# Seven norms of a two-block kernel: squares summed with a token per partition, the row spread by a matmul with the identity

## The reference, cut to what matters

```python
def rms_norm(x, g):
    xf = x.astype(jnp.float32)
    y = xf * lax.rsqrt(jnp.mean(xf * xf, axis=-1, keepdims=True) + EPS)
    return (y * g.astype(jnp.float32)).astype(x.dtype)
```

## Time and profile before

| | |
|---|---|
| median of three runs | 2040.0 us |
| the profiled execution | 2036.15 us |
| its span in the profile | 2034.4 us |
| PE busy, DVE, ACT, POOL | 1922.1, 991.6, 758.7, 111.9 us |
| mean granted clock of PE | 0.981 of full |
| read from HBM | 280.84 MB, 139 GB/s over the span |

### The profile page before, as it was taken

How to read it: one execution, slowest core, us unless ns; L and a number is a source line. 1 busy time by engine, 2 the same in 40 slices (tenths; PEclk the granted TensorE clock), 3 DMA queues, 4 the chain that set the end, 5 groups by cost and what they waited for, 6 DMA issues and landing times.

```text
span 2034.4 us, 28356 instructions
## 1 busy us (share of the span) xinstructions
PE 1922.1 (94%) x11844; PEld 1661.3 (82%) x11844; DVE 991.6 (49%) x1126; ACT 758.7 (37%) x918; POOL 111.9 (6%) x106
## 2 busy tenths in 40 slices
PE   7999998899997999888999999999989989989998
PEld 6989896798985768767887788887867767989997
DVE  5555465554556426664233522223245475554454
ACT  5334435433444424164222412213234435344343
POOL 3000201200022000000000100000001010000000
PEclk9999999999998999899999999999999999999999
DMA  9996387498433312001323232332324211556641
GB/s 255 323 309 233 116 310 254 141 335 259 176 124 125 116 59 85 19 1 62 104 83 103 62 103 83 103 103 83 103 78 153 73 62 49 180 145 180 183 176 61
DMA packets 288755, 283.47 MB, mean 139 GB/s; under 512 B 8760, under 2 KB 265669, under 8 KB 282515
## 3 DMA queue, kind: packets, MB, share of 16 engines
q1 hardware_dynamic: 287312, 279.56, 43.6%
q0 software_dynamic: 1120, 2.46, 0.4%
q10 hardware_dynamic: 227, 0.06, 0.0%
HBM read 280.84 MB, written 1.07 MB: 139 GB/s over the span
## 4 chain that ended last, share of the span: by engine, by line
PE 84%; DVE 8%; ACT 5%; POOL 1%; issue 1%; DMA 1%; ACTq 0%; SPq 0%; DVEq 0%
PE PS L1516 24%; PE PS L1518 23%; PE PS L1517 23%; PE PS L1612 2%; PE PS L1601 2%; PE PS L2007 1%; DVE WLO L951 1%; PE PS L1861 1%; PE PS L1995 1%; PE PS L1957 1%; PE PS L1970 1%; ACT WHI L591 1%; DVE RT L989 1%; POOL X L546 1%; ACT PB L860 1%
## 5 line engine op out<-in xcount | busy, mean ns | idle before, releaser
L1516 PE MATMUL PS<-AHI,WHI 128*128 128x256 f32 (+1 forms) x2480 | 801.1, 323 | 45.8 <-DVE ALO L1217 18.6
L1517 PE MATMUL PS<-ALO,WHI 128*128 128x256 f32 (+1 forms) x2480 | 787.8, 318 | 0.0
L1518 PE MATMUL PS<-AHI,WLO 128*128 128x256 f32 (+1 forms) x2480 | 787.3, 317 | 0.0
L951 DVE TENSOR_TENSOR WLO<-RAW,WHI 128x2048 fp32r<-128x2048 f32 x210 | 485.0, 2311 | 431.3 <-ACT WHI L591 431.3
L1516 PEld LDWEIGHTS PS<-AHI,WHI 128*128 128x128 f32 x2480 | 480.6, 194 | 114.5 <-issue 51.8
L591 ACT ACTIVATE WHI<-RAW 128x2048 fp32r<-128x2048 f32 x210 | 400.4, 1908 | 284.5 <-PE PS L1518 266.8
L1517 PEld LDWEIGHTS PS<-ALO,WHI 128*128 128x128 f32 x2480 | 481.2, 194 | 30.3 <-issue 1.7
L1518 PEld LDWEIGHTS PS<-AHI,WLO 128*128 128x128 f32 x2480 | 480.5, 194 | 29.0
L1516 PE MATMUL PS<-SHI,WHI 128*128 128x256 f32 (+1 forms) x704 | 221.3, 314 | 2.3 <-DVE HB L1493 2.3
L1518 PE MATMUL PS<-SHI,WLO 128*128 128x256 f32 (+1 forms) x704 | 218.0, 310 | 0.0
L1517 PE MATMUL PS<-SLO,WHI 128*128 128x256 f32 (+1 forms) x704 | 217.9, 310 | 0.0
(11 more groups left out here) (248 smaller groups left out, 1723.2 us busy)
## 6 DMA issues: line engine op xcount, KB each, us to landing
RAW<-in_w_in_dram SPq DMA_DIRECT2D x98, 512.0 KB, 4.5
MRAW<-in_w_mod_dram SPq DMA_DIRECT2D x48, 1024.0 KB, 7.2
RAW<-in_ffn_w_gu_dram SPq DMA_DIRECT2D x88, 512.0 KB, 7.6
RAW<-in_w_gate_up_dram SPq DMA_DIRECT2D x88, 512.0 KB, 5.0
RAW<-in_ffn_w_down_dram SPq DMA_DIRECT2D x44, 512.0 KB, 4.3
RAW<-in_w_down_dram SPq DMA_DIRECT2D x44, 512.0 KB, 4.0
RAW<-in_w_out_dram SPq DMA_DIRECT2D x24, 512.0 KB, 4.6
RAW<-in_w_o_attn_dram SPq DMA_DIRECT2D x16, 512.0 KB, 4.2
```

The lines of the kernel that those rows point to most:

```text
L951: dve.tensor_tensor(WLO[:, c % RING, :], RAW[:, c % RING, :], WHI[:, c % RING, :].bitcast(F32), ALU.subtract)\
L1516: pe.matmul(out, whi, xhi, start=first, stop=False, skip_group_check=shared)
L1517: pe.matmul(out, whi, xlo, start=False, stop=False, skip_group_check=shared)
L1518: return pe.matmul(out, wlo, xhi, start=False, stop=last, skip_group_check=shared)
```

## The change

For norms 3, 7, 8, 9, 10, 11 and 12 (`ROW_BANK`):
- `norm_sums` makes the squares the stationary operand and one column of ones the moving one, once per block of 128 tokens. The sums land in PSUM as 128x2 or 128x4 numbers, a token per partition. Per k that is two or four one-column matmuls instead of one of 256 or 512 columns.
- `norm_std` takes the root of these numbers into the new tile `RTOK`, `norm_row` their reciprocal.
- PE spreads the result (`norm_rows`): per block of tokens a matmul with `RTOK`'s column, repeated over 128 columns, as the stationary operand and the identity as the moving one. It waits for the reciprocal, and stands right behind the last sums in PE's order, in norm 3 ahead of the sixteen modulation matmuls.
- DVE waits for the spread and reads the row from PSUM (`rms_row`) in its products. In norms 8 to 10 ACT copies the context's row to `RT` for POOL; the second reciprocal after the seventh product is gone, and so are the two separate roots.

The other six norms stay as they were.

```diff
+ROW_BANK = {3: 0, 7: 3, 8: 6, 9: 6, 10: 6, 11: 6, 12: 6}
+CTX_BANK = {8: 5, 9: 7, 10: 7}
+ROWS_DONE = {n: i + 1 for i, n in enumerate(ROW_BANK)}
...
+        RTOK = sm("RTOK", [P, 4])
...
+        def rms_row(n_norm):
+
+            return PS[:, ROW_BANK[n_norm], 0:TX] if n_norm in ROW_BANK else RT[:, 0:TX]
...
             def norm_std(n_norm, t):
 
                 act.wait_ge(S("n_ss"), n_norm + 1)
-                act.activation(RT[:, 0:P * t], stat_row(n_norm, t), ACT.Sqrt, scale=1.0 / D, bias=EPSC[:, 0:1])\
-                   .then_inc(S("n_std"), 1)
+                if n_norm in ROW_BANK:
+                    act.activation(RTOK[:, 0:t], PS[:, STAT_BANK[n_norm], 0:t], ACT.Sqrt, scale=1.0 / D, bias=EPSC[:, 0:1])\
+                       .then_inc(S("n_std"), 1)
+                else:
+                    act.activation(RT[:, 0:P * t], stat_row(n_norm, t), ACT.Sqrt, scale=1.0 / D, bias=EPSC[:, 0:1])\
+                       .then_inc(S("n_std"), 1)
+                if n_norm in CTX_BANK:
+
+                    act.wait_ge(S("n_bc"), ROWS_DONE[n_norm])
+                    act.activation(RT[:, TX:TB], PS[:, CTX_BANK[n_norm], 0:TX], ACT.Copy).then_inc(S("n_rtc"), 1)
...
             def norm_row(n_norm, t):
 
                 dve.wait_ge(S("n_std"), n_norm + 1)
+                if n_norm in ROW_BANK:
+                    dve.reciprocal(RTOK[:, 0:t], RTOK[:, 0:t]).then_inc(S("n_rt"), 1)
+                    dve.wait_ge(S("n_bc"), ROWS_DONE[n_norm])
+                    return
...
             def modulated(n_norm, inst, a_inst, which, shift, t):
 
                 halves = t // 2
-                if halves == 1:
-                    norm_row(n_norm, t)
-                else:
-                    dve.wait_ge(S("n_stdx"), inst + 1)
-                    dve.reciprocal(RT[:, 0:TX], RT[:, 0:TX]).then_inc(S("n_rt"), 1)
-                    dve.wait_ge(S("n_rt"), n_norm + 1)
+                norm_row(n_norm, t)
...
-                                             in1=RT[:, 0:TX], op0=ALU.mult, op1=ALU.mult).then_inc(S("xm"), 1)
-                    if k == 6 and halves == 2:
-                        dve.wait_ge(S("n_std"), n_norm + 1)
-                        dve.reciprocal(RT[:, TX:TB], RT[:, TX:TB]).then_inc(S("n_rtc"), 1)
+                                             in1=rms_row(n_norm), op0=ALU.mult, op1=ALU.mult).then_inc(S("xm"), 1)
...
                 for k in ks:
                     pe.wait_ge(S("n_sq"), KT * n_norm + k + 1)
-                    last = pe.matmul(stat_row(n_norm, t), ONES[:, :], src[:, k, 0:P * t], start=k == 0, stop=k == KT - 1)
+                    if n_norm in ROW_BANK:
+                        for a in range(t):
+                            last = pe.matmul(PS[:, STAT_BANK[n_norm], a:a + 1], src[:, k, a * P:a * P + P], ONES[:, 0:1],
+                                             start=k + a == 0, stop=k == KT - 1, skip_group_check=True)
+                    else:
+                        last = pe.matmul(stat_row(n_norm, t), ONES[:, :], src[:, k, 0:P * t], start=k == 0, stop=k == KT - 1)
...
+            def norm_rows(n_norm):
+
+
+                t = n_stat(n_norm)
+                pe.wait_ge(S("n_rt"), n_norm + 1)
+                for a in range(t):
+                    bank = ROW_BANK[n_norm] if a < 2 else CTX_BANK[n_norm]
+                    last = pe.matmul(PS[:, bank, a % 2 * P:a % 2 * P + P], RTOK[:, a:a + 1].broadcast_to([P, P]), IDENT[:, :],
+                                     start=True, stop=True)
+                last.then_inc(S("n_bc"), 1)
...
                 norm_sums(3, 2, SQ1, range(4, KT))
+                norm_rows(3)
                 modulation(32, 33, 34, 35)
```

More of the change, by code:

```diff
@@ L750, in modulated @@
                 squares(lambda k: X[:, k, 0:n], lambda k: SQ2[:, k, 0:n], ready, range(squared, KT))
[L751 to L756, removed]
-                else:
-                    norm_std(n_norm, t)
+                norm_std(n_norm, t)
                 for k in range(KT):
@@ L997, in gained_lo, with branch @@
                        .then_inc(S("act_lo"), 1)
-            def branch(src, gain, inst=None, name=None):
+            def branch(src, gain, n_norm, inst=None, name=None):
                 for k in range(KT):
-                    dve.scalar_tensor_tensor(out=TU[:, k, :], in0=src(k), scalar=gain(k), in1=RT[:, 0:TX],
+                    dve.scalar_tensor_tensor(out=TU[:, k, :], in0=src(k), scalar=gain(k), in1=rms_row(n_norm),
                                              op0=ALU.mult, op1=ALU.mult).then_inc(S("xt"), 1)
@@ L1080, in _ @@
                 dve.wait_ge(S("hg"), 2)
-                branch(lambda k: acc(k, TX), lambda k: HG[:, inst, k:k + 1], *((1, "attn_pre_g"), (4, "ple_pre_g"))[inst])
+                branch(lambda k: acc(k, TX), lambda k: HG[:, inst, k:k + 1], post, *((1, "attn_pre_g"), (4, "ple_pre_g"))[inst])
                 if inst == 1:
@@ L1177, in _ @@
                 dve.wait_ge(S("f_ev"), 4)
-                branch(lambda k: FB[:, k, :], lambda k: par("attn_post_g", k), 3, "ffn2_pre_g")
+                branch(lambda k: FB[:, k, :], lambda k: par("attn_post_g", k), 3, 3, "ffn2_pre_g")
             split_w(None, FIRST["ple_proj"] + AHEAD)
@@ L1201, in _ @@
             dve.wait_ge(S("f_ev"), 8)
-            branch(lambda k: FB[:, k, :], lambda k: par("ple_post_g", k))
+            branch(lambda k: FB[:, k, :], lambda k: par("ple_post_g", k), 7)
             split_w(None, FIRST["ple_gate"] + 3 + AHEAD)
@@ L1503, in _ @@
             for k in range(KT):
-                dve.scalar_tensor_tensor(out=YF[:, k, :], in0=X[:, k, 0:TX], scalar=par("norm_final_2", k), in1=RT[:, 0:TX],
+                dve.scalar_tensor_tensor(out=YF[:, k, :], in0=X[:, k, 0:TX], scalar=par("norm_final_2", k), in1=rms_row(12),
                                          op0=ALU.mult, op1=ALU.mult).then_inc(S("yf"), 1)
@@ L1827, in _ @@
             norm_sums(7, 2, SQ1, range(2, KT))
+            norm_rows(7)
             for layer in range(2):
@@ L1865, in _ @@
                 norm_sums(8 + 2 * layer, 4, SQ2, range((0, 6)[layer], KT))
+                norm_rows(8 + 2 * layer)
                 beside = [lambda: network(0), lambda: network(1), lambda: network(2), lambda: taps(0), lambda: taps(1),
@@ L2071, in _ @@
                 norm_sums(9 + 2 * layer, nt // P, SQ2, range(4, KT))
+                norm_rows(9 + 2 * layer)
                 inst = 2 + layer
@@ L2088, in _ @@
             norm_sums(12, 2, SQ1, range(6, KT))
+            norm_rows(12)
             pe.wait_ge(S("xd"), 3 * KT)
```

## The result

The changed kernel takes 2047.64 us (median of 6 runs, 2046.37 to 2051.43) beside 2039.21 us for the kernel before, timed beside it: a ratio of 1.0047, with a 95% interval of 1.0037 to 1.0057. It is slower by 8.4 us. The forecast was 2045 us (2031 to 2053), 4.8 us more than before, with a half chance of slower.

A forecast was written before the change was run, and what follows sets the result against it. TensorE, busy 94% of the span, was taken as the bound. The norms' terms (-2.6+3.6+2.4+2.5-0.5-0.6) summed to +4.8 us: 2041.0 for the profiled execution, 2045 us against the median, range 2031 to 2053.

The forecast's parts named there:

- main mechanism: One-column sums hardly hold or lift TensorE's clock; norm 8's would run at half throughout, 13.1 us against 9.07.
- The chain: Root to first product in a norm: 1.34 us for two tiles (0.95 gained), 1.77 for four (0.5 gained).
- Sums equal at full clock: At full clock, one-column matmuls per k take the same time as the old wide one: nothing gained or lost.
- Norm 3: Shorter chain, and faster products and adds with the row in PSUM: -2.6 us; -0.9 if only the chain counts.
- Norms 7 and 8: Norm 7 -0.3; norm 8's sums at half clock +4.0, its spread +0.3, the rest -0.4: +3.6 us together.
- Norm 9: Low clock behind the first sum batch +2.5, slow spread +0.2, second reciprocal gone -0.3: +2.4 us.
- Norm 10: Low clock where sums alternate with down-projection +3.2, chain and second reciprocal -0.7: +2.5 us.
- rival (b): Clock fails only in norm 8; norm 9's first batch and norm 10's alternation hold it: -0.9 us, 2039; 22%.
- Rival (c): Norm 10's clock stays down until the stage ends, 13 us instead of one or two stretches: 2053; 8%.
- Norms 11 and 12: Norm 11: shorter chain less a longer low stretch, -0.5 us; norm 12: shorter chain without cover, -0.6 us.
- Rival (a): One-column work keeps the clock, so all seven norms gain: -10.5 us, 2029.5; 20%.
- Rival (d): The row in PSUM doesn't speed VectorE: norm 3 -0.9 instead of -2.6 us; no chance of its own given.

The follow-up runs named there:

- w128_all: The changed kernel with all seven norms' sums multiplied by 128 columns of ones instead of one; 2030.4 us, 7.8 us faster than the kernel before.
- narrow_8: w128_all with norm 8's sums alone back to one column; that stage cost 5.2 us more than in w128_all.
- narrow_7: w128_all with norm 7's sums alone back to one column; 2.3 us more than w128_all over the stage of norms 7 and 8.
- w128_8: The changed kernel with 128 columns of ones in norm 8's sums alone; gained 5.8 us by the medians.
- row_sbuf: w128_all with the spread row copied by ScalarE from PSUM to SBUF before VectorE reads it, all seven norms; 2041.66 us, 1.0012 to the kernel before.
- fill: w128_all with 2 to 7 unused matmuls of ones behind the spread of norms 8 to 12; 2026.0 us.
- w128_9_10: The changed kernel with 128 columns of ones in the sums of norms 9 and 10 alone; gained 8.2 us on the changed kernel.
- fill_7: fill with seven more unused matmuls of ones behind norm 7's spread; median not lower than fill's, filled kernels came to 2026 to 2028.4 us.

## Why the prediction was right

The time (2045 forecast, 2047.6 measured), the sign and the main mechanism held: one-column sums at 0.50 in norm 8, 13.81 us against the 13.1 computed from the earlier trace rows. The forecast change was +4.8 us and the medians give +8.4; in the profiles the seven norms sum to +5.0, and what is left lies in stages that the forecast put at nothing. Point by point:

- **The chain.** Forecast 1.34 us for two tiles and 1.77 for four at full clock; measured in w128_all, where the clock is full, 1.27 and 1.72, and in the changed kernel's norm 3 1.63, its spread slow. The bound from the earlier trace rows (0.74 us for the spread of two tiles) was met by 0.71.
- **Sums equal at full clock.** At full clock the sums of one k cost the same in either form. From the timelines of norm 10, the kernel before and then the changed one:

```profile
1503.67 1.02 PE L1612 MATMUL PS<-SQ,ONES 128*128 128x512 f32 x2
```

```profile
1525.62 0.95 PE L1619 MATMUL PS<-ONES,SQ 128*128 128x1 f32 x8
```

  So the loss at the sums is the clock's.
- **Norm 3, -2.6: -2.45 measured.** The chain and the adds gave their 0.7 and 1.8 us. A low stretch within the narrow sums, which the step did not have, took some 0.3 back (w128_all, with wide sums, has -2.72).
- **Norms 7 and 8, +3.6: +4.5 measured,** but with a cause that I had wrong in part. I took the clock to be low in norm 8 anyway, and read its old sums as begun at half. They began at full: in the kernel before the clock stood at 1.00 while PE was idle ahead of them (636.3 to 640.6 us) and over their first 0.3 us:

```profile
636.30:640.60 4.30, 0.00 (x0) 1.00 0.00 0
640.64:640.95 0.31, 0.31 (x1) 1.00 0.00 0
```

  narrow_8 and narrow_7 show that it is norm 7's 16 narrow matmuls that bring it down before norm 8 begins, and norm 8's own that would bring it down if norm 7's did not. The step also took VectorE's products in norm 8 to have two SBUF inputs; they read the row from PSUM, and only the low parts have two.
- **Norm 9, +2.4: +1.4 measured.** The stretch came, 3.4 us at 1138, 1.2 us behind the first batch, over wide matmuls without a gap: 1.7 us, where I took 2.5. The one behind the norm was longer than before, 10.2 us. In w128_8 the same code cost nothing (-0.09), so the size is no more than this execution's.
- **Norm 10, +2.5: +2.9 measured.** The clock fell in the alternation of wide and narrow work and came back by itself once, as the forecast had it. That it fell was in part luck: in w128_8 the same alternation held the clock, as rival (b) had it, and the norm came to -1.88. Rival (c), never coming back, did not occur (and was priced at +8, where its own terms, 13 in place of 3.2, give nearly 10).
- **Norms 11 and 12, -0.5 and -0.6: -0.35 and -1.0.**
- **Rival (a), -10.5 us,** is what the changed kernel would have been with a clock that holds. w128_all built just that: 7.8 us under the kernel before, -12.4 us over the norms in its profile. Its terms came out at norm 3 -2.7 (-2.7 forecast), norms 7 and 8 -2.6 (-2.9), norm 9 -1.9 (-1.5), norm 10 -3.2 (-1.5), norms 11 and 12 -0.9 and -1.0 (-0.95 each).
- **Rival (d), that the row in PSUM brings nothing,** fell with row_sbuf. I had counted this gain in norm 3 only; in the modulated norms it is at least as large (3.3 and 3.4 us in norms 9 and 10, the copy and the longer low clock included; norm 8 was forecast "between -2 and +1; -0.4").

By the rule of the Trainium skill that the prediction weighed (TensorE: Matmul & The Clock Gate, HAM oscillation), idle gaps between bursts cost the clock. fill agrees: 1.7 us of matmuls in a gap kept the clock at 1.00 behind norms 8, 9 and 10. narrow_8 disagrees that gaps are the whole of it: the clock fell 2.1 us into 11.9 us without any gap.

What stays open: how much each norm is worth in the median, and why the stages without an edit come out 0.7 to 9.1 us behind the kernel before in the table. Its rather quick profiled execution accounts for up to 3.1 of them. The rest follows neither form nor source of the row: between the norms fill and w128_9_10, which read the row from PSUM, come to -0.5 and +1.1, and fill_7 and w128_all, which do so too, to +5.6 and +6.6. Their low stretches fell elsewhere; whether by chance or because the work reached them at another time, no run tells, since none shifted those stages alone.

## What to carry to other kernels

Where TensorE bounds a kernel, a matmul made narrower is not made cheaper: look at its duration per instruction first, which here was the same for 1 and for 128 columns, and then at the granted clock over it and behind it. If narrow work must stand for some microseconds without a gap, write more columns than you need and read one, and fill the wait behind it with matmuls into a bank that is about to be overwritten; but do this where TensorE, not another engine, is the one that the next stage waits for. And read operands from PSUM rather than SBUF on VectorE where GpSimd works beside it.

## What the runs showed of the hardware that I had not expected

- The clock falls from full within gapless one-column matmuls, 2.1 us after they began in narrow_8, and stays at 0.50 for 20.5 us, until wide matmuls have run. In turn with wide matmuls such sums held it for over 13 us in norm 10 of w128_8 and did not in the changed kernel.
- Within norm 7's last eight one-column matmuls (2.8 us in narrow_7) the clock falls for 10.2 us, over idle time and wide work alike; at norm 3's it was 3.4 us.
- A product of 128x256 on VectorE with both inputs in SBUF takes 0.95 us beside a GpSimd add, and 0.47 us with one input in PSUM.
- The runs of one kernel can spread much wider than another's: w128_8 from 2033.8 to 2048.9 us, the kernel before from 2036.9 to 2043.2. No run shows why; that its norms 9 and 10 sit where the clock can fall either way is a guess.
